# A gated recurrence in 64-wide chunks: the transposed inverse of row tile 1 kept in the other half of the partitions, and output sums taken part by part

## The reference, cut to what matters

```python
def wkv7_scan(r, w, k, v, a, b):
    # per head, state S (B,H,Nv,Nk):
    # S_t = S_{t-1} diag(w_t) + (S_{t-1} a_t) b_t^T + v_t k_t^T ;  y_t = S_t r_t
    def step(state, inp):
        r_t, w_t, k_t, v_t, a_t, b_t = inp
        sa = jnp.einsum('bhvk,bhk->bhv', state, a_t)
        state = (state * w_t[:, :, None, :] + sa[..., None] * b_t[:, :, None, :]
                 + v_t[..., None] * k_t[:, :, None, :])
        return state, jnp.einsum('bhvk,bhk->bhv', state, r_t)
```

## Time and profile before

| | us |
|---|---|
| median of 3 runs | 1905.72 (1900.38 to 1912.37) |
| profiled execution, first to last instruction (its span) | 1904.3 |
| lies around the span, taken as the difference to the median | 1.4 |
| TensorE busy in it | 1878.8 |
| VectorE, ScalarE, GpSimd busy | 1198.5, 1007.6, 91.6 |
| recurrence stage of the first mixer, in the span | 345 to 620 |

### The profile page before, as it was taken

How to read it: one execution, slowest core, us unless ns; L and a number is a source line. 1 busy time by engine, 2 the same in 40 slices (tenths; PEclk the granted TensorE clock), 3 DMA queues, 4 the chain that set the end, 5 groups by cost and what they waited for, 6 DMA issues and landing times.

```text
span 1904.3 us, 31110 instructions
## 1 busy us (share of the span) xinstructions
PE 1878.8 (99%) x12720; PEld 1599.7 (84%) x12720; DVE 1198.5 (63%) x2473; ACT 1007.6 (53%) x2054; POOL 91.6 (5%) x187
## 2 busy tenths in 40 slices
PE   9999999999999999999999999999999999999998
PEld 7888888888888788888888887888888888878887
DVE  5576555666654656766675765667565757656565
ACT  5565554423312555645565666556555656665554
POOL 0000000212210000010000000000000000000000
PEclk9999999999989999999999999999999999999999
DMA  6555443122202355635463342556355733435552
GB/s 237 188 210 210 178 155 111 68 96 71 71 30 96 114 205 178 251 106 195 177 250 113 130 151 94 178 195 251 125 177 179 261 104 129 149 111 188 185 189 112
DMA packets 42717, 296.12 MB, mean 156 GB/s; under 512 B 4832, under 2 KB 4960, under 8 KB 10576
## 3 DMA queue, kind: packets, MB, share of 16 engines
q1 hardware_dynamic: 41184, 288.32, 42.6%
q0 software_dynamic: 1392, 5.83, 0.9%
HBM read 293.08 MB, written 1.05 MB: 154 GB/s over the span
## 4 chain that ended last, share of the span: by engine, by line
PE 94%; DVE 3%; ACT 1%; POOL 1%; issue 1%; DMA 0%; SPq 0%; POOLq 0%; DVEq 0%; ACTq 0%
PE PS L1605 21%; PE PS L1547 16%; PE PS L1549 15%; PE PS L1548 15%; PE PS L1607 11%; PE PS L1556 1%; PE PS L2049 1%; PE PS L1825 1%; PE PS L1844 1%; PE PS L1837 1%; PE PS L1582 1%; PE PS L1741 1%; PE PS L1961 1%; DVE wlo L2453 1%; PE PS L2038 1%
## 5 line engine op out<-in xcount | busy, mean ns | idle before, releaser
L2453 DVE TENSOR_TENSOR wlo<-raw,whi 128x512 fp32r<-128x512 f32 (+5 forms) x784 | 614.2, 826 | 199.1 <-ACT whi L2092 193.0
L1605 PE MATMUL PS<-xhl,whi 128*128 128x512 f32 x1728 | 613.4, 399 | 0.0
L2092 ACT ACTIVATE whi<-raw 128x512 fp32r<-128x512 f32 (+5 forms) x784 | 533.4, 735 | 142.5 <-PE PS L1549 139.2
L1607 PE MATMUL PS<-xhl,wlo 128*128 128x256 f32 x1728 | 485.0, 281 | 0.0
L1605 PEld LDWEIGHTS PS<-xhl,whi 128*128 128x128 f32 x1728 | 324.7, 188 | 79.4
L1607 PEld LDWEIGHTS PS<-xhl,wlo 128*128 128x128 f32 x1728 | 326.3, 189 | 2.1
L1547 PE MATMUL PS<-whi,yh 128*128 128x512 f32 (+2 forms) x572 | 225.7, 395 | 0.0
L1548 PE MATMUL PS<-wlo,yh 128*128 128x512 f32 (+2 forms) x572 | 221.9, 388 | 0.0
L1549 PE MATMUL PS<-whi,yl 128*128 128x512 f32 (+2 forms) x572 | 221.8, 388 | 0.0
L2538 DVE TENSOR_TENSOR arena<-arena,PS 128x256 f32<-128x256 f32 x216 | 90.2, 418 | 159.5 <-ACT arena L2162 159.5
L1547 PE MATMUL PS<-whi,xhl 128*128 128x512 f32 (+4 forms) x480 | 189.6, 395 | 0.5 <-DVE wlo L2453 0.3
(11 more groups left out here) (273 smaller groups left out, 2519.0 us busy)
## 6 DMA issues: line engine op xcount, KB each, us to landing
raw<-wall SPq DMA_DIRECT2D x249, 1024.0 KB, 4.9
raw<-wall SPq DMA_DIRECT2D x12, 768.0 KB, 4.2
raw<-wall SPq DMA_DIRECT2D x8, 968.0 KB, 4.9
raw<-wall SPq DMA_DIRECT2D x4, 896.0 KB, 4.6
arena<-ebias POOLq DMA_DIRECT2D x2, 768.0 KB, 4.6
raw<-wall SPq DMA_DIRECT2D x2, 720.0 KB, 4.4
raw<-wall SPq DMA_DIRECT2D x2, 640.0 KB, 4.2
X<-x SPq DMA_DIRECT2D x2, 512.0 KB, 6.1
```

What stands on the lines that cost most here:

```text
L1605: e.matmul(b, hi[:, c0:c0 + 128], xhl[:, k, :, :].rearrange("p a t -> p (a t)"), start=(k == 0), stop=False, skip_group_check=True)
L1607: p = e.matmul(b[:, 0:256], lo[:, c0:c0 + 128], xh[:, k, :], start=False, stop=(k == 7), skip_group_check=True)
L2092: e.activation(whi[slot_of(i)][:, c].bitcast(F32R), raw[i % 3][:, c], copy).then_inc(*M.sig("whi", ("split", i, q)))
L2453: e.tensor_tensor(wlo[slot_of(i)][:, c], raw[i % 3][:, c], whi[slot_of(i)][:, c].bitcast(F32), ALU.subtract).then_inc(*M.sig("wlo", *[("ha ...
```

## The change: what it does

- `units()` now gives each product a second half cs beside ps: cs = q for row tile 0, and 1 - q for row tile 1. `DT`, `X` and `AG` of row tile 1 are kept with their halves exchanged. So `r_x` and `r_g0` read ps and write cs; `r_dm0`, `Dd` and `r_w` read cs and write ps; `Dt` reads and writes cs. For row tile 1 the products use rows 0 with columns 1, and rows 1 with columns 0.
- Each of these steps but `Dt` writes to two banks that are neighbours, one per row tile. `take_two` and `room_for_two` hand out neighbouring banks; ScalarE and VectorE read both banks in one instruction.
- `r_yp` runs over the four parts outside and over hh and q inside, so that consecutive products go to different quarters (one line now, 28 products).
- `u` is 2 tt + hh in place of 2 hh + tt. `r_dt` is 1 multiplication on 128 partitions and 2 on 64 in place of 2 on 128; the copy of `AG` in `r_ka` is 3 instructions (1 on 128 partitions, 2 on 64) in place of 1.
- The masks m1 to m5 are stored twice as wide: the second load of constants is 1506 columns in place of 1186.
- `PACE` has smaller TensorE numbers for the steps concerned, and with the bank rules this gives another order of the whole stage. Of the 272 fill matmuls 268 are left (those ahead of `r_rp` of group 7 find no free bank).

```diff
-    "r_masks": (("dve", 1.4),), "r_dt": (("dve", 1.0),), "r_dm0": (("pe", 0.5), ("act", 0.4)), "r_g0": (("pe", 0.5), ("act", 0.4)),
-    "r_x": (("pe", 0.5),), "r_xc": (("dve", 0.3),), "r_d": (("pe", 0.95),), "r_dd": (("dve", 0.6),),
-    "r_w": (("pe", 0.9), ("act", 0.6)), "r_rp": (("pe", 0.6), ("dve", 0.95)), "r_yp": (("pe", 1.6),),
+    "r_masks": (("dve", 1.4),), "r_dt": (("dve", 1.0),), "r_dm0": (("pe", 0.35), ("act", 0.4)), "r_g0": (("pe", 0.35), ("act", 0.4)),
+    "r_x": (("pe", 0.35),), "r_xc": (("dve", 0.3),), "r_d": (("pe", 0.8),), "r_dd": (("dve", 0.6),),
+    "r_w": (("pe", 0.6), ("act", 0.6)), "r_rp": (("pe", 0.6), ("dve", 0.95)), "r_yp": (("pe", 1.1),),
...
+    def neighbours(self):
+        order = {i: n for n, (i, _) in enumerate(self.free)}
+        found = [(max(order[i], order[i + 1]), i) for i in order if i + 1 in order]
+        return min(found)[1] if found else None
+
+    def take_two(self, first, second):
+        i = self.neighbours()
+        for key, at in ((first, i), (second, i + 1)):
+            self.at[key] = next(f for f in self.free if f[0] == at)
+            self.free.remove(self.at[key])
...
             def units():
                 for hh in range(2):
                     for tt in range(2):
                         for q in range(2):
-                            yield hh, tt, 2 * hh + tt, slice(64 * q, 64 * q + 64)
+                            c = 1 - q if tt else q
+                            yield hh, tt, 2 * tt + hh, slice(64 * q, 64 * q + 64), slice(64 * c, 64 * c + 64)
...
-                b, W_ = bank(("r_x", g, k)), WH[slot("whole", g)]
-                for t in due(bank_free(("r_x", g, k)), ("act", ("Dm0", g)), k > 1 and ("dve", ("Dm", g, k - 1))):
+                b, W_ = both("r_x", g, k), WH[slot("whole", g)]
+                for t in due(*both_free("r_x", g, k), ("act", ("Dm0", g)), k > 1 and ("dve", ("Dm", g, k - 1))):
                     e.wait_ge(*t)
-                for hh, tt, u, ps in units():
-                    p = e.matmul(b[ps, u * 32:(u + 1) * 32], W_.T[ps, hh, 0, tt, 0:64], some(W_.Dm[ps, u, :], k, 0),
-                                 start=True, stop=True)
+                for hh, tt, u, ps, cs in units():
+                    p = e.matmul(PS[cs, b[tt], hh * 32:hh * 32 + 32], W_.T[ps, hh, 0, tt, 0:64],
+                                 some(W_.Dm[ps, u, :], k, 0), start=True, stop=True)
...
                 for tt in range(2):
-                    for hh in range(2):
-                        for q in range(2):
-                            b, ps, h = bank(("YP", g, q)), slice(64 * q, 64 * q + 64), slice(64 * hh, 64 * hh + 64)
...
+                    for part in range(4):
+                        for hh in range(2):
+                            for q in range(2):
+                                b, ps, h = bank(("YP", g, q)), slice(64 * q, 64 * q + 64), slice(64 * hh, 64 * hh + 64)
+                                u, v = 2 * tt + hh, slice(tt * 128 + hh * 64, tt * 128 + hh * 64 + 64)
+                                if part > 1 and (tt, q) == (1, 1):
+                                    continue
+                                o = b[h, 128 * (part // 2) + tt * 64:128 * (part // 2) + tt * 64 + 64]
```

More of the change, by code:

```diff
@@ L179, in const_table @@
     for k in range(1, 6):
-        put(f"m{k}", lower(k))
+        put(f"m{k}", np.tile(lower(k), (1, 2)))
     f = np.float32
@@ L523, in room, with room_for_two @@
         while len(self.bank.free) < n:
+            yield 1
+    def room_for_two(self):
+        while self.bank.neighbours() is None:
             yield 1
@@ L864, in free, with pair @@
                 self.bank.give((step, g) + a)
+            def pair(step, *a):
+                self.bank.take_two(*[(step, g) + a + (tt,) for tt in range(2)])
+                self.do(step, s, g, *a)
+                for tt in range(2):
+                    self.bank.give((step, g) + a + (tt,))
             while not fronts.free:
@@ L925, in group @@
             yield 1
-            yield from self.room(1)
-            one("r_dm0")
-            free("r_dm0")
-            yield from self.room(1)
-            one("r_g0")
-            free("r_g0")
+            yield from self.room_for_two()
+            pair("r_dm0")
+            yield from self.room_for_two()
+            pair("r_g0")
             yield 1
@@ L934, in group @@
                 self.do("r_xz", s, g, k)
-                yield from self.room(1)
-                one("r_x", k)
+                yield from self.room_for_two()
+                self.bank.take_two(*[("r_x", g, k, tt) for tt in range(2)])
+                self.do("r_x", s, g, k)
                 yield 1
                 self.do("r_xc", s, g, k)
-                free("r_x", k)
+                for tt in range(2):
+                    self.bank.give(("r_x", g, k, tt))
                 yield 1
-                yield from self.room(2)
+                while not (len(self.bank.free) >= 3 and self.bank.neighbours() is not None or k == 5 and self.bank.free):
+                    yield 1
                 if k < 5:
-                    self.bank.take(("Dd", g, k))
+                    self.bank.take_two(*[("Dd", g, k, tt) for tt in range(2)])
                 self.bank.take(("Dt", g, k))
@@ L949, in group @@
                 if k < 5:
-                    free_d = ("Dd", g, k)
-                    self.bank.give(free_d)
+                    for tt in range(2):
+                        self.bank.give(("Dd", g, k, tt))
                 self.bank.give(("Dt", g, k))
                 yield 1
-            yield from self.room(1)
-            one("r_w")
-            free("r_w")
+            yield from self.room_for_two()
+            pair("r_w")
             yield 1
@@ L1377, in bank, with both, banks, freed @@
             return PS[:, P.bank.at[tile][0], :]
+        def both(*tile):
+            a, b = [P.bank.at[tile + (tt,)][0] for tt in range(2)]
+            assert b == a + 1
+            return a, b
+        def banks(*tile):
+            a, b = both(*tile)
+            return PS[:, a:b + 1, :]
+        def freed(*tile):
+            return [("free", tile + (tt,)) for tt in range(2)]
+        def both_free(*tile):
+            return [bank_free(tile + (tt,)) for tt in range(2)]
         def bank_free(tile):
@@ L2293, in r_dm0 @@
                     e.wait_ge(*t)
-                e.activation(WH[slot("whole", g)].Dm, u4(bank(("r_dm0", g))[:, 0:256]), copy).then_inc(
-                    *M.sig("act", ("Dm0", g), ("free", ("r_dm0", g))))
+                e.activation(u2(flat(WH[slot("whole", g)].Dm)), banks("r_dm0", g)[:, :, 0:128], copy).then_inc(
+                    *M.sig("act", ("Dm0", g), *freed("r_dm0", g)))
             def r_g0(s, g):
@@ L2299, in r_g0 @@
                     e.wait_ge(*t)
-                e.activation(WH[slot("whole", g)].AG[:, :, :, 1, :],
-                             bank(("r_g0", g))[:, 0:256].rearrange("p (h t k) -> p h t k", h=2, t=2), copy).then_inc(
-                    *M.sig("act", ("g0", g), ("free", ("r_g0", g))))
+                e.activation(WH[slot("whole", g)].AG[:, :, 1, :].rearrange("p (t h) k -> p t h k", t=2),
+                             banks("r_g0", g)[:, :, 0:128].rearrange("p t (h k) -> p t h k", h=2), copy).then_inc(
+                    *M.sig("act", ("g0", g), *freed("r_g0", g)))
             def r_w(s, g):
@@ L2306, in r_w @@
                     e.wait_ge(*t)
-                e.activation(WH[slot("whole", g)].W1, u4(bank(("r_w", g))), copy).then_inc(
-                    *M.sig("act", ("w", g), ("free", ("r_w", g))))
+                e.activation(u2(flat(WH[slot("whole", g)].W1)), banks("r_w", g)[:, :, 0:256], copy).then_inc(
+                    *M.sig("act", ("w", g), *freed("r_w", g)))
             def r_ys(s, g):
```

102 lines of the change are left out of this document (50 added, 52 removed).

## The result

| | us |
|---|---|
| kernel before, measured beside it | 1900.39 (1898.99 to 1912.91, 11 runs) |
| changed kernel | 1917.07 (1913.16 to 1921.29, 11 runs) |
| ratio | 1.0071, 95% interval 1.0053 to 1.0088 |
| forecast | 1882.6, range 1867 to 1900 |
| profiled execution of the changed kernel | 1917.34, span 1915.5 |

The time lies 17 us above the range's upper end. It is 0.7% slower, so of my three cases "within 1%" (0.36) is the one that came, at its far side.

The account below looks back on a forecast made before the run. It took TensorE to bound the kernel: 1904.3 - 32 (quarters) + 8 (waits) + 0.4 (constants) + 0.9 (`r_dt`) - 0.4 (fills) = 1881.2 us of span, with 1.4 around it 1882.6 us; range 1867 to 1900.

Parts of the forecast that it names:

- within 1%: Whole kernel: time differs by no more than about 1% (19 us) from before, either way; chance 0.36.
- TensorE is the bound: Recurrence stage: time is TensorE's, 99% busy over the span, so shortening what it issues pays if the others keep up.
- Steps with four quarters, 2.55 + 0.38 us a group: `r_dm0`, `r_g0`, `r_x`, `Dd`: 11 steps save 2.55 us a group going from two quarters to four; `r_w` saves 0.38.
- `r_yp`, 1.09 us a group: Output sums `r_yp`: turning to another quarter with each product takes 0.93 us, 1.09 us less a group.
- Sum of 32 us: Recurrence stage: all TensorE savings together, 4.0 us a group over 8 groups.
- issue is the bound: Rival: issuing products limits TensorE, so narrow steps gain nothing; about 1901 us, chance 0.10.
- banks give no gain: Rival: neighbouring banks or the row-tile rule hold chains up, so no step gets shorter; 1907 us, chance 0.05.
- I add 8 us, from 3 to 15: Recurrence stage: new TensorE waits on VectorE from the new order, 8 us, range 3 to 15.
- The same cold stretch: Part of the stage without dense products: clock at 0.50 for the same 13.6 us as before, no change in cost.
- Fills, constants, `r_dt`: 0.4, 0.4 and 0.9 us: 4 fills less save 0.4 us; the larger constants load adds 0.4; the additional `r_dt` instruction adds 0.9.
- The time turns into waits: Rival: VectorE becomes the bound in part and half of the 32 us comes back; 1891 us, chance 0.14.
- Slower: Rival: narrow products and waits keep the clock low much longer late in the stage; about 1916 us, chance 0.05.

Follow-up runs that it names:

- e3: Kernel before with only the `r_yp` loops exchanged, so consecutive products use different quarters; 1898.7 us, ratio 0.9967.
- e10: Changed kernel with one VectorE step, `r_st` of group 5, moved ahead of the work it stood behind; 1914.7 us.
- e1: Changed kernel with the order of steps of the kernel before replayed (11 steps come later); 1902.9 us.
- e5: Kernel before, old products, with `PACE` numbers searched anew for it, giving another order; 1905.5 us.
- e12: Kernel before with 18 fill matmuls more, ahead of the 2.1 us wait at `r_dm0` of group 6; 1900.4 us.
- e9: Kernel before with only the changed kernel's smaller TensorE numbers in `PACE`; 1921.5 us.
- e6: Changed kernel, same order, with 188 more fill matmuls ahead of 18 steps with TensorE's largest waits; 1912.4 us.
- e7: Changed kernel re-ordered by searched `PACE` numbers, with 73 more fill matmuls ahead of eight of the re-ordered kernel's waits; 1884.8 us.

## Why the prediction was wrong, step by step

- *"TensorE is the bound", "nothing hides it".* Right for the kernel before (5.5 us of waits in 293.4). With the change 35.9 of 307.4 us are waits.
- *Steps with four quarters, 2.55 + 0.38 us a group.* Right: spacing 0.25 us for `Dd` as forecast, busy 0.45 us for `r_x` (18.1/40), 0.68 for `r_w` (forecast 0.72), but 0.50 for `r_dm0` (forecast 0.43 to 0.45). The rule on row tiles and banks from the Trainium skill's page "TensorEngine Tiling (Array Packing)", section "Restrictions and Gotchas", doesn't bind here: the 16 records of a `Dd` begin within 0.25 us, which at 58 ns a record in one quarter takes all four at once, so both row halves in each of its two banks.
- *`r_yp`, 1.09 us a group.* 16.4 to 9.3 us in the rows is 0.89 a group; e3 gave 7.7 us in all for 8.7. The forecast was slightly too high.
- *Sum of 32 us.* 30.0 measured in the account. This part of the forecast held, and so the rivals "issue is the bound" and "banks give no gain" fell.
- *"I add 8 us, from 3 to 15".* This step failed first: the waits grew by 30.4 us. The count laid TensorE's work between a result and its reader beside a way through VectorE, with what else stands in its queue only at a few places. It left out that a pair of banks must be free (`r_x` behind L2890), that ScalarE has a queue too (5.2 us of the stage's waits end with one of its instructions, none did before), and that a late step makes the next late. It named the right end of the stage: the 4 us from `r_yp` of group 7 on were 4.6, and at `r_dm0` of group 6 it had 2 us, where 0.6 came, but 4.4 at the `r_s` of group 5 just ahead of it, whose `r_st` stood in the same queue (e10). What it had least of was the stretch beside the streamed projections: of its 11 us some 3 were left for that, and 19.7 came from 345 to 545 us. The count that walks all engines in order, made after the result, gives 51.5 us for the changed list and 16.8 for the old one, 34.7 apart, where the traces are 30.4 apart. It could have been made before the run, from the same rows and the order. It is no fine measure: for e1 it gave 23.2 more than for before, where the traces have 15.5, and it missed e5.
- *"The same cold stretch".* Failed: 13.7 became 41.0 us, in seven pieces and not one, for 13.6 us. And the 13.7 were not a fixed part of the kernel before (e12): against its usual executions the clock costs some 17 to 19 us more, which is the whole of the slowdown. I had tied the clock to the missing dense products; it also fell in the middle of the streamed projections, at 365.8 us for 13.7 us, behind waits of 0.5 us or less and ahead of one of 2.0, and at 420 and 434, where waits of 1.2 to 1.4 us follow each other.
- *Fills, constants, `r_dt`: 0.4, 0.4 and 0.9 us.* Too small to be told from the rest. TensorE's first wait for weights is 0.62 us in place of the 1.87 of the earlier trace rows, but that is no gain: in the profiles with the smaller load it goes from 1.0 to 1.9 us, in those with the larger one from 0.6 to 2.4. The larger load is not seen in it.
- *The rivals.* "The time turns into waits" had the mechanism and half its size: all of the gain came back, not 16 us. "Slower" had the clock as its second half, but at another place. It was given 0.05, because its price was taken from one long stretch beside `wout` and not from many short ones. Two of the prediction's own signs of being wrong came, waits above 16 us and a clock below 1 in more of the stage.
- *The changed numbers.* The prediction named them as a cause of "another order" and put no price on that. e9 puts 21 us on it with every instruction unchanged.

What stays open: how the pairs cost 19.4 us, whether by waiting for banks (as most of the 10.6 us ahead of `r_x` do) or by yet another order that was not chosen for its steps; and what decides in a single execution whether the clock falls at a place.

## What to carry to other kernels

When an order has been fitted to the lengths of its steps, a change of the lengths, or of the planner's numbers alone, is a change of the order: price it by walking every engine's queue and every buffer through the new list, not by looking at single hand-overs. A gain per instruction should be tried in the old order and in one fitted anew before it is judged; here the same quarters gave 1917, 1903, 1898 and 1889 us, and 1885 with fills. And a wait of TensorE can be paid twice, as time and again in clock. Fills in the waits brought the clock back, but took most of it again as work: 5, 4 and 0 us of the medians were left in e6, e7 and e12, where a better order was worth 28. So order first, and filler only where the trace shows the wait, in no greater number than the wait holds.

## What was not expected of the hardware

- Short waits cost clock: with some 40 waits of 0.2 to 4.4 us in the stage, the granted clock was 0.50 for 41.0 us, in pieces of 3.4 to 13.7 us, though TensorE was busy for 76 to 96% of each slice. With 188 fills ahead of waits (e6) it was 6.8 us.
- The clock differs between executions of one kernel. e1's ten runs reach from 1893.9 to 1909.9 us, with mean clocks from 0.997 down to 0.985. Before spread over 10.6 us beside e12, and e12 with its one filled wait over 1.9. Filling is not needed for a small spread, nor does it always give one: e5, without fills, spread over 2.5 us, e6, with 188, over 5.1.
